# Prompt values of the first two key tiles: three products of rounded numbers and remainders in place of one native float32 product

## The chip, the cores and the metric

The kernel runs on one core of one Trainium2 chip. The metric is the device time of one launch in microseconds (us). TensorE (PE) multiplies into PSUM, VectorE (DVE) and ScalarE (ACT) work on PSUM and SBUF, GpSimd (POOL) on SBUF, and SyncE (SP) issues most transfers.

## The reference

One inference step of a decoder with a gated short-convolution layer and a latent-attention layer, for a prompt of 512 tokens and 8 sample sequences of 8 new tokens each (against 1024 cached ones), model width 2048, 16 heads. The part that the change touches is the prompt's causal attention and its values:

```python
def prompt_latent_attention(q_lat, q_pe, ckv, kpe):
    ...
        p = jax.nn.softmax(sc, axis=-1).astype(ckv.dtype)
        return jnp.einsum('bhqk,bkc->bqhc', p, ckv)
...
def mla_output(o_lat, z, w_kv_up, w_out):
    b, t = o_lat.shape[:2]
    o = jnp.einsum('bthc,chv->bthv', o_lat, w_kv_up[..., QK_NOPE_DIM:]).reshape(b, t, D_ATTN)
    return (o * jax.nn.silu(z)) @ w_out
```

The kernel computes the same thing for the prompt in another order: it first expands the latent into keys and values per head (V = ckv times the value half of w_kv_up), then multiplies the 512 values of a head by its probabilities.

## The kernel before

A float32 number can be fed to PE in two ways. As `F32` it is multiplied natively. As `F32R` PE takes a rounded number; for full precision the kernel then stores a rounded part (hi) and a remainder (lo) and adds three products, hi x hi, hi x lo and lo x hi. Nearly all of the kernel is done in the second way. The prompt's values, the transposes and the sample queries are native.

The prompt's attention runs over `Fori(0, H // G)`: four groups of G = 4 heads. A group makes queries (query_tiles, L1307), keys (key_tiles, L1277) and values (value_tiles, L1291) of its heads, and then goes through the heads. PE's order is written out by hand:

```python
                value_tiles(n + 5, 1)
                scores(1)
                turn_probs(0)
                scores(2)
                values(0)
                turn_probs(1)
                scores(3)
                values(1)
                turn_probs(2)
                sample_queries(0)
                sample_queries(1)
                values(2)
                turn_probs(3)
                sample_queries(2)
                sample_queries(3)
                values(3)
```

For a head j:
- scores(j) (L1336): for each of QT = 4 query tiles i, five rounded products into PSUM bank i, over (i + 1) x 128 keys. Bank i must have been read by the exponentials of head j - 1 (`exp_done`).
- maxima(j) on DVE (L2737): mask of the diagonal block, then the row maximum, for each i; it raises `bias_ready`.
- exps(j) on ACT (L1956): the exponential of each i into `PROBS[j % 2]` with the row sum; it raises `exp_done`. For j >= 2 the buffer must be free, which before the change means that the transposes of head j - 2 are done (`tr_done`).
- normalise(j) on DVE (L2747): reciprocal and four scalings of the probabilities, then `p_ready`.
- turn_probs(j) on PE (L1353): the ten 128 x 128 blocks of the causal triangle are transposed into PSUM banks 4 to 6.
- evac(j) on ACT (L1965): three copies of those banks into `PT` (`pt_evac`).
- values(j) on PE (L1369): for each key tile k = 0 to 3 one native product of 128 values by the probabilities of the query tiles k to 3, that is 512, 384, 256 and 128 columns, accumulated in PSUM bank 7; then `pv_done`. Bank 7 must have been read by out(j - 1) (`o_done`).
- out(j) on DVE (L2756): bank 7 times the gate.
- sample_queries(j) on PE (L1326) takes `WK[j]`, which SP loads (load_wk, L684), one semaphore for each of four buffers.

DVE's order in a group is: remainders of queries and keys, then for j = 0 to 3 maxima(j), normalise(j) and for j >= 2 out(j - 2); then sample_query(0), sample_query(1), out(2), sample_query(2), sample_query(3), out(3). ACT's is: exps(0), two roundings of weights, four copies of PSUM banks 4 to 7 into `V` (L1977, `v_evac`), then exps(1), evac(0), exps(2), evac(1), exps(3), evac(2), evac(3). Engines work through their lists strictly in order, so an instruction that waits holds all behind it.

Of the kernel before, what the change touches and what calls it, by code (L numbers as in the profile page):

```python
# [45 lines left out]
G = 4  # L46
# [105 lines left out]
def build(nc, wstream, adastream, x_in, small_in, cos_in, sin_in, pages, ptab, wk_in, wv_in,  # L152
          y_out, cst_out, ckv_out, kpe_out, rope_park, y_park):
    with ExitStack() as ctx:
# [106 lines left out]
        PROBS = [at(f"probs{i}", ro + 10 * P * i, [P, 10 * P]) for i in range(2)]  # L261
        PRS = at("probs_sample", to, [P, PAST])
# [154 lines left out]
        wk_landed = [sem(f"wk_landed{i}") for i in range(G)]  # L417
# [32 lines left out]
        def _(sp):  # L450
# [233 lines left out]
            def load_wk(h, s):  # L684
                sp.dma_start(WK[s][:, :], wk_in[bass.ds(h, 1), :, :].rearrange("a p n -> p (a n)")).then_inc(wk_landed[s], 16)
# [23 lines left out]
            def group_loads(g, n, last):  # L709
# [11 lines left out]
                for j in range(0 if last else G):  # L721
                    sp.wait_ge(qlat_done, g * G + (j + 1))
                    load_wk(g * G + (j + G), j)
# [99 lines left out]
        def _(pe):  # L823
# [451 lines left out]
            with pe.Fori(0, H // G) as g:  # L1275
# [50 lines left out]
                def sample_queries(j):  # L1326
# [3 lines left out]
                    pe.wait_ge(wk_landed[j], g * 16 + 16)  # L1330
# [22 lines left out]
                def turn_probs(j):  # L1353

                    pe.wait_ge(p_ready, g * G + (j + 1))
                    if j == 0:
                        pe.wait_ge(v_evac, g * G + G)
                    else:
                        pe.wait_ge(pt_evac, g * 12 + 3 * j)
                    s = 0  # L1360
# [8 lines left out]
                def values(j):  # L1369
                    pe.wait_ge(o_done, g * G + (j + BEGUN))  # L1370
                    s = 0
                    for k in range(QT):
                        if k < 3:
                            pe.wait_ge(pt_evac, g * 12 + (3 * j + k + 1))
                        w = QT - k
                        last = pe.matmul(PS[:, 7, k * P:TP], V[:, k, j * VD:(j + 1) * VD], PT[:, s * P:(s + w) * P],  # L1376
                                         start=(k == 0), stop=(k == QT - 1))
                        s += w
                    last.then_inc(pv_done, 1)
# [169 lines left out]
        def _(act):  # L1549
# [389 lines left out]
            with act.Fori(0, H // G) as g:  # L1939
# [16 lines left out]
                def exps(j):  # L1956
                    if j >= 2:
                        act.wait_ge(tr_done, g * 12 + 3 * (j - 1))
# [6 lines left out]
                def evac(j):  # L1965
                    for c in range(3):
                        w = 4 * P if c < 2 else 2 * P
                        act.wait_ge(tr_done, g * 12 + (3 * j + c + 1))
                        act.activation(PT[:, 4 * c * P:4 * c * P + w], PS[:, 4 + c, 0:w], ACT.Copy).then_inc(pt_evac, 1)
# [6 lines left out]
                for t in range(QT):  # L1976
                    act.activation(V[:, t, :], PS[:, 4 + t, :], ACT.Copy).then_inc(v_evac, 1)  # L1977
# [81 lines left out]
        def _(dve):  # L2059
# [676 lines left out]
            def group(g, last=False):  # L2736
# [18 lines left out]

                def out(j):  # L2756
# [18 lines left out]
                for j in range(G):  # L2775
                    maxima(j)
                    normalise(j)
                    if j >= 2:
# [3 lines left out]
                out(2)  # L2782
                sample_query(2)
# [281 lines left out]
```

## Time and profile before

| | |
|---|---|
| median of 3 runs | 2016.57 us (2015.34 to 2018.63) |
| profiled execution | 2017.29 us |
| its span, first to last instruction | 2015.6 us |
| mean granted TensorE clock | 0.992 |
| PE busy | 1951.2 us (97%) |
| DVE busy | 1421.8 us (71%) |
| ACT busy | 848.1 us (42%) |
| POOL busy | 172.3 us (9%) |

The span is what the profile sees; the execution's own time is 1.7 us longer. Times in the rows count from the first instruction. An engine is busy while one of its instructions runs; ends of pipelined matmuls are modelled, so the step from one start to the next is the better measure of what a matmul costs. The granted clock of TensorE has two levels here, 1.00 (2.4 GHz) and 0.50 (1.2 GHz).

### The profile page before, as it was taken

To read this page: it belongs to the slowest core of one execution; us is meant where nothing else is said; L and a number is where in the kernel's file an instruction comes from. 1 tells how busy PE (TensorE), PEld (TensorE's weight loads), DVE (VectorE), ACT (ScalarE), POOL (GpSimd) and SP (SyncE) were. 2 spreads that over 40 slices of the span, in tenths; PEclk is the share of its full clock that TensorE was granted. 3 is DMA by queue.
4 is the path that set the end of the run, shared out by engine and by line. 5 is a ranking of instruction groups with operands and counts; after the bars stand their busy time and mean duration, and the time that the engine had idled before them with its cause. 6 is when DMAs were issued, how large, how long until landed. Compare 5 with 4: busy or idle time off the path is not lost.

```text
span 2015.6 us, 42249 instructions
## 1 busy us (share of the span) xinstructions
PE 1951.2 (97%) x16142; PEld 1836.6 (91%) x16142; DVE 1421.8 (71%) x2077; ACT 848.1 (42%) x1318; POOL 172.3 (9%) x124
## 2 busy tenths in 40 slices
PE   4999999999999999999999999998999999999997
PEld 3899999999999999999999999998888887779996
DVE  5597777777777777797778986676434456669776
ACT  3243333333333333354455634445443444456443
POOL 1200000000000000000000240003221122200002
PEclk8999999999999999999999999999999999999998
DMA  9976555555555565645453434448323239852447
GB/s 392 404 267 210 201 193 193 193 195 204 202 205 198 205 202 197 235 165 159 142 210 138 165 130 139 140 136 299 117 73 94 76 107 347 289 186 96 137 149 282
DMA packets 134902, 386.69 MB, mean 192 GB/s; under 512 B 13906, under 2 KB 44498, under 8 KB 131858
## 3 DMA queue, kind: packets, MB, share of 16 engines
q1 hardware_dynamic: 129682, 368.52, 53.1%
q0 software_dynamic: 5120, 16.78, 2.7%
q8 instruction: 69, 1.13, 0.2%
q14 instruction: 31, 0.25, 0.0%
HBM read 353.92 MB, written 31.33 MB: 191 GB/s over the span
## 4 chain that ended last, share of the span: by engine, by line
PE 82%; DVE 8%; DMA 6%; issue 2%; ACT 1%; SPq 1%; DVEq 0%; ACTq 0%
PE ps L954 36%; PE ps L958 18%; DMA s<-adastream 4%; PE ps L906 3%; PE ps L1435 3%; PE ps L840 3%; PE ps L1286 2%; PE ps L1301 2%; PE ps L1461 2%; PE ps L1319 2%; PE ps L1376 2%; PE ps L892 1%; PE ps L847 1%; DMA w_raw<-wstream 1%; DVE w_split L2177 1%
## 5 line engine op out<-in xcount | busy, mean ns | idle before, releaser
L1617 ACT ACTIVATE w_split<-w_raw 128x1024 fp32r<-128x1024 f32 x204 | 216.0, 1059 | 381.3 <-PE ps L958 207.6
L2177 DVE TENSOR_TENSOR w_split<-w_raw,w_split 128x1024 fp32r<-128x1024 f32 x212 | 259.6, 1224 | 139.2 <-ACT w_split L1617 134.5
L954 PE MATMUL ps<-operand_hi,w_split 128*128 128x288 f32 x1224 | 328.5, 295 | 0.0
L954 PE MATMUL ps<-operand_lo,w_split 128*128 128x288 f32 x1224 | 328.3, 294 | 0.0
L954 PE MATMUL ps<-t_hi,w_split 128*128 128x288 f32 x960 | 262.9, 300 | 1.2 <-ACT w_split L1617 0.7
L954 PE MATMUL ps<-t_lo,w_split 128*128 128x288 f32 x960 | 258.0, 295 | 0.0
L784 POOL TENSOR_TENSOR w_split<-w_raw,w_split 128x1024 fp32r<-128x1024 f32 x47 | 126.3, 2687 | 1509.4 <-ACT w_split L1555 1509.4
L954 PEld LDWEIGHTS ps<-operand_hi,w_split 128*128 128x128 f32 x1224 | 229.7, 188 | 0.1
L954 PEld LDWEIGHTS ps<-operand_lo,w_split 128*128 128x128 f32 x1224 | 229.7, 188 | 0.0
L954 PEld LDWEIGHTS ps<-t_hi,w_split 128*128 128x128 f32 x960 | 180.3, 188 | 10.7 <-issue 8.9
L958 PE MATMUL ps<-operand_hi,w_split 128*128 128x288 f32 x1224 | 186.9, 295 | 0.9 <-DVE w_split L2177 0.9
L954 PE MATMUL ps<-t_hi_out,w_split 128*128 128x288 f32 x672 | 182.2, 297 | 4.8 <-DVE t_lo_out L2430 1.9
L954 PE MATMUL ps<-t_lo_out,w_split 128*128 128x288 f32 x672 | 180.5, 295 | 0.0
L954 PEld LDWEIGHTS ps<-t_lo,w_split 128*128 128x128 f32 x960 | 180.3, 188 | 0.0
L958 PEld LDWEIGHTS ps<-operand_hi,w_split 128*128 128x128 f32 x1224 | 170.2, 188 | 1.5 <-DVE w_split L2177 1.5
L1617 ACT ACTIVATE w_split<-a 128x1024 fp32r<-128x1024 f32 x88 | 93.4, 1061 | 185.1 <-PE ps L958 185.1
L958 PE MATMUL ps<-t_hi,w_split 128*128 128x288 f32 x960 | 146.2, 294 | 0.0
L954 PEld LDWEIGHTS ps<-t_hi_out,w_split 128*128 128x128 f32 x672 | 126.2, 188 | 9.3 <-issue 8.6
L958 PEld LDWEIGHTS ps<-t_hi,w_split 128*128 128x128 f32 x960 | 133.1, 188 | 0.0
L954 PEld LDWEIGHTS ps<-t_lo_out,w_split 128*128 128x128 f32 x672 | 126.2, 188 | 0.0
L2177 DVE TENSOR_TENSOR w_split<-a,w_split 128x1024 fp32r<-128x1024 f32 x88 | 107.4, 1220 | 25.3 <-ACT w_split L1617 25.2
L1555 ACT ACTIVATE w_split<-w_raw 128x1024 fp32r<-128x1024 f32 (+1 forms) x62 | 64.0, 1033 | 130.8 <-PE ps L1319 40.9
(412 smaller groups left out, 3896.6 us busy)
## 6 DMA issues: line engine op xcount, KB each, us to landing
w_raw<-wstream SPq DMA_DIRECT2D x169, 512.0 KB, 3.7
ada_ring<-adastream SPq DMA_DIRECT2D x112, 512.0 KB, 4.6
a<-wstream SPq DMA_DIRECT2D x88, 512.0 KB, 4.7
s<-wstream SPq DMA_DIRECT2D x44, 512.0 KB, 3.4
ada_first_ring<-adastream SPq DMA_DIRECT2D x32, 512.0 KB, 9.2
ada_third<-adastream SPq DMA_DIRECT2D x32, 512.0 KB, 6.4
tiles<-y_park SPq DMA_DIRECT2D x12, 1152.0 KB, 7.3
x_residual<-x_in SPq DMA_DIRECT2D x8, 1152.0 KB, 8.7
```

The source lines that it names most:

```text
L784: pool.tensor_tensor(WL[:, n.slot, 0:width], WR[:, n.slot, 0:width], WH[:, n.slot, 0:width].bitcast(F32), ALU.subtract).then_inc(w_lo_read ...
L840: pe.matmul(PS[0:cols, banks[a], 0:HALF], WH[:, c.slot, kk * cols:(kk + 1) * cols], x[:, k * T + a * HALF:k * T + (a + 1) * HALF], start=( ...
L906: last = pe.matmul(PS[32 * g:32 * g + 32, bank, col:col + P], small("c", 32 * k, 32), w, start=(clears and k == 0), stop=(k == KT - 1), sk ...
L954: pe.matmul(PS[:, bank, 0:HALF], WH[:, c.slot, k * P:(k + 1) * P], x(k), start=(first and k == 0 and x is hi), stop=False, skip_group_chec ...
L958: done = pe.matmul(PS[:, bank, 0:HALF], WL[:, c.slot, k * P:(k + 1) * P], hi(k), start=False, stop=(last and k == HK - 1), skip_group_chec ...
L1286: last = pe.matmul(PS[:, 2 * c + jj, :], w[:, nn.slot, k * 256 + jj * P:k * 256 + (jj + 1) * P], x[:, k * TP:(k + 1) * TP], start=(w is WH ...
L1301: last = pe.matmul(PS[:, 4 + t, :], x[:, k * TP + t * P:k * TP + (t + 1) * P], w[:, nn.slot, kk * 512:(kk + 1) * 512], start=(w is WH and ...
L1319: last = pe.matmul(PS[:, 4 * c + 2 * jj + a, 0:HALF], w[:, nn.slot, k * 256 + jj * P:k * 256 + (jj + 1) * P], x[:, k * T + a * HALF:k * T ...
L1435: pe.matmul(*form(c, k, slice(0, P)), start=(k == 0), stop=False)
L1555: act.activation(WH[:, n.slot, 0:width], WR[:, n.slot, 0:width], ACT.Copy).then_inc(w_hi_ready, 1)
L1617: act.activation(WH[:, c.slot, :], raw, ACT.Copy).then_inc(w_hi_ready, 1)
L2177: dve.tensor_tensor(WL[:, c.slot, :], raw, WH[:, c.slot, :].bitcast(F32), ALU.subtract).then_inc(w_lo_ready, 1)
```

## The change

In values(j), the products of key tiles 0 and 1 are now made of rounded parts: `VH` (values, rounded by ACT when it copies them from PSUM) and `VL` (their remainder), `PTH` (transposed probabilities, rounded by ACT) and `PTL` (their remainder). Key tiles 2 and 3 stay native. With it:
- DVE gets values_low(), four subtractions of 256 columns in each group, between normalise(0) and maxima(1), and probs_low(j), two subtractions of 512 and 384 columns for each head, between normalise(j + 1) and the next out, and for the last head behind out(2).
- ACT's evac(j) copies four pieces, since bank 5 holds columns of both kinds.
- PE waits for `v_lo` before turn_probs(0), since that overwrites the banks from which values_low() reads, and for `p_lo` at the head of values(j).
- `PTL[0]` and `PTL[1]` lie in the memory of `PROBS[0]` and `PROBS[1]`. So exps(j) now waits for values(j - 2) to be done, where it waited for the transposes of head j - 2.
- The four semaphores `wk_landed` become two, each for a pair of `WK` buffers. SP loads the buffers in pairs.

```diff
--- before.py
+++ after.py
@@ -259,6 +259,11 @@
         T2 = at("tmp2", to + T, [P, T])
         ACC = at("acc", to + 2 * T, [P, T])
         PROBS = [at(f"probs{i}", ro + 10 * P * i, [P, 10 * P]) for i in range(2)]
+        PTH = at("probs_t_hi", xo, [P, 7 * P], F32R)
+        PTL = [at(f"probs_t_lo{i}", ro + 10 * P * i, [P, 7 * P], F32R) for i in range(2)]
+        VH = at("values_hi", po + 10496, [P, 2, G * VD], F32R)
+        VL = [[at(f"values_lo{k}{i}", o, [P, 2 * VD], F32R) for i, o in enumerate(places)]
+              for k, places in enumerate(((xo + 4352, po + 14080), (ro + 20 * P, mo + CT * P)))]
         PRS = at("probs_sample", to, [P, PAST])
         PRN = at("probs_new", to + PAST, [P, TS])
         RA21 = at("a21", to, [P, CH])
@@ -414,7 +419,7 @@
         qpe_landed = sem("qpe_landed")
         ckv_stored, ckv_back = sem("ckv_stored"), sem("ckv_back")
         q_hi, q_lo, k_hi, k_lo = sem("q_hi"), sem("q_lo"), sem("k_hi"), sem("k_lo")
-        wk_landed = [sem(f"wk_landed{i}") for i in range(G)]
+        wk_landed, v_lo, p_lo = [sem(f"wk_landed{i}") for i in range(2)], sem("v_lo"), sem("p_lo")
         v_evac = sem("v_evac")
         qlat_done, qlat_evac = sem("qlat_done"), sem("qlat_evac")
         score_done, bias_ready, exp_done, p_ready = sem("score_done"), sem("bias_ready"), sem("exp_done"), sem("p_ready")
@@ -682,7 +687,7 @@
                     b1_back(8 + 4 * g, 12 + 4 * g)
 
             def load_wk(h, s):
-                sp.dma_start(WK[s][:, :], wk_in[bass.ds(h, 1), :, :].rearrange("a p n -> p (a n)")).then_inc(wk_landed[s], 16)
+                sp.dma_start(WK[s][:, :], wk_in[bass.ds(h, 1), :, :].rearrange("a p n -> p (a n)")).then_inc(wk_landed[s // 2], 16)
 
             def load_rope(g, turns, s):
 
@@ -719,7 +724,7 @@
                     sp.wait_ge(rope_parked[1], 128)
                     load_rope(g + 1, 2, 0)
                 for j in range(0 if last else G):
-                    sp.wait_ge(qlat_done, g * G + (j + 1))
+                    sp.wait_ge(qlat_done, g * G + (j // 2 * 2 + 2))
                     load_wk(g * G + (j + G), j)
 
             with sp.Fori(0, H // G - 1) as g:
@@ -1327,7 +1332,7 @@
 
 
                     pe.wait_ge(exp_done, g * 16 + (4 * (G - 1) + j + 1))
-                    pe.wait_ge(wk_landed[j], g * 16 + 16)
+                    pe.wait_ge(wk_landed[j // 2], g * 32 + 32)
                     for k in range(CT):
                         last = pe.matmul(PS[:, j, k * P:(k + 1) * P], WK[j][:, k * P:(k + 1) * P],
                                          QNS[:, j, :], start=True, stop=True)
@@ -1355,8 +1360,10 @@
                     pe.wait_ge(p_ready, g * G + (j + 1))
                     if j == 0:
                         pe.wait_ge(v_evac, g * G + G)
+                        pe.wait_ge(v_lo, g * 2 + 2)
                     else:
                         pe.wait_ge(pt_evac, g * 12 + 3 * j)
+                        pe.wait_ge(p_lo, g * G + j)
                     s = 0
                     for k in range(QT):
                         for i in range(k, QT):
@@ -1368,14 +1375,21 @@
 
                 def values(j):
                     pe.wait_ge(o_done, g * G + (j + BEGUN))
+                    pe.wait_ge(p_lo, g * G + (j + 1))
                     s = 0
                     for k in range(QT):
                         if k < 3:
                             pe.wait_ge(pt_evac, g * 12 + (3 * j + k + 1))
-                        w = QT - k
-                        last = pe.matmul(PS[:, 7, k * P:TP], V[:, k, j * VD:(j + 1) * VD], PT[:, s * P:(s + w) * P],
-                                         start=(k == 0), stop=(k == QT - 1))
-                        s += w
+                        c = slice(s * P, (s + QT - k) * P)
+                        v = slice(j * VD, (j + 1) * VD)
+                        if k < 2:
+                            low = VL[k][j // 2][:, j % 2 * VD:(j % 2 + 1) * VD]
+                            terms = ((VH[:, k, v], PTH[:, c]), (VH[:, k, v], PTL[j % 2][:, c]), (low, PTH[:, c]))
+                        else:
+                            terms = ((V[:, k, v], PT[:, c]),)
+                        for i, (value, prob) in enumerate(terms):
+                            last = pe.matmul(PS[:, 7, k * P:TP], value, prob, start=(k == 0 and i == 0), stop=(k == QT - 1))
+                        s += QT - k
                     last.then_inc(pv_done, 1)
 
                 pe.wait_ge(qlat_evac, g * G + BEGUN)
@@ -1955,7 +1969,7 @@
 
                 def exps(j):
                     if j >= 2:
-                        act.wait_ge(tr_done, g * 12 + 3 * (j - 1))
+                        act.wait_ge(pv_done, g * G + (j - 1 + BEGUN))
                     for i in range(QT):
                         o, w = P * (i * (i + 1) // 2), (i + 1) * P
                         act.wait_ge(bias_ready, g * 16 + (4 * j + i + 1))
@@ -1966,7 +1980,12 @@
                     for c in range(3):
                         w = 4 * P if c < 2 else 2 * P
                         act.wait_ge(tr_done, g * 12 + (3 * j + c + 1))
-                        act.activation(PT[:, 4 * c * P:4 * c * P + w], PS[:, 4 + c, 0:w], ACT.Copy).then_inc(pt_evac, 1)
+                        high = (w, 3 * P, 0)[c]
+                        if high:
+                            last = act.activation(PTH[:, 4 * c * P:4 * c * P + high], PS[:, 4 + c, 0:high], ACT.Copy)
+                        if high < w:
+                            last = act.activation(PT[:, 4 * c * P + high:4 * c * P + w], PS[:, 4 + c, high:w], ACT.Copy)
+                        last.then_inc(pt_evac, 1)
 
                 for s in range(2):
                     act.wait_ge(rope_parked[s], 128)
@@ -1974,7 +1993,7 @@
                 for c in range(2):
                     round_w(n + (4 + c))
                 for t in range(QT):
-                    act.activation(V[:, t, :], PS[:, 4 + t, :], ACT.Copy).then_inc(v_evac, 1)
+                    act.activation((VH if t < 2 else V)[:, t, :], PS[:, 4 + t, :], ACT.Copy).then_inc(v_evac, 1)
                 for j in range(1, G):
                     exps(j)
                     evac(j - 1)
@@ -2753,6 +2772,22 @@
                         last = dve.tensor_scalar(pr, pr, MX[:, 12 + i:13 + i], None, ALU.mult)
                     last.then_inc(p_ready, 1)
 
+                def values_low():
+                    for k in range(2):
+                        dve.wait_ge(v_evac, g * G + (k + 1))
+                        for i in range(2):
+                            c = slice(2 * i * VD, 2 * (i + 1) * VD)
+                            last = dve.tensor_tensor(VL[k][i][:, :], PS[:, 4 + k, c], VH[:, k, c].bitcast(F32), ALU.subtract)
+                        last.then_inc(v_lo, 1)
+
+                def probs_low(j):
+                    dve.wait_ge(tr_done, g * 12 + (3 * j + 3))
+                    for c, w in enumerate((4 * P, 3 * P)):
+                        dve.wait_ge(pt_evac, g * 12 + (3 * j + c + 1))
+                        o = slice(4 * c * P, 4 * c * P + w)
+                        last = dve.tensor_tensor(PTL[j % 2][:, o], PS[:, 4 + c, 0:w], PTH[:, o].bitcast(F32), ALU.subtract)
+                    last.then_inc(p_lo, 1)
+
                 def out(j):
                     dve.wait_ge(pv_done, g * G + (j + 1 + BEGUN))
                     o = B1[:, bass.ds(g * (G * T) + j * T, TP)]
@@ -2775,11 +2810,16 @@
                 for j in range(G):
                     maxima(j)
                     normalise(j)
+                    if j == 0:
+                        values_low()
+                    else:
+                        probs_low(j - 1)
                     if j >= 2:
                         out(j - 2)
                 sample_query(0)
                 sample_query(1)
                 out(2)
+                probs_low(3)
                 sample_query(2)
                 sample_query(3)
                 if last:
```

## Rows read from the trace of the kernel before

**Rows 1.** The page: busy time of PE, and shares of the chain that ended last, by engine.

```profile
PE 1951.2 (97%) x16142; PEld 1836.6 (91%) x16142; DVE 1421.8 (71%) x2077; ACT 848.1 (42%) x1318; POOL 172.3 (9%) x124
...
PE 82%; DVE 8%; DMA 6%; issue 2%; ACT 1%; SPq 1%; DVEq 0%; ACTq 0%
```

**Rows 2.** Windows, one group's tail: length, busy us of PE, PEld, DVE, ACT, POOL, clock, DMA.

```profile
1438.64:1464.89 26.25, 26.24 (x166) 22.07 (x164) 16.70 (x46) 15.22 (x41) 2.40 (x1) 1.00 0.36 93
```

**Rows 3.** Timeline of PE there: start us, us, engine, line, operation, tiles, count.

```profile
1444.44 0.34 PE L1347 MATMUL ps<-k_nope_hi,q_nope_lo 128*128 128x384 f32 x1
1444.61 0.34 PE L1348 MATMUL ps<-k_nope_lo,q_nope_hi 128*128 128x384 f32 x1
...
1445.15 0.40 PE L1346 MATMUL ps<-k_nope_hi,q_nope_hi 128*128 128x512 f32 x1
1445.38 0.40 PE L1347 MATMUL ps<-k_nope_hi,q_nope_lo 128*128 128x512 f32 x1
...
1446.31 2.32 PE L1376 MATMUL ps<-probs_t,values 128*128 128x512 f32 x8
1448.47 1.26 PE L1364 MATMUL ps<-small,probs 128*128 128x128 f32 x10
...
1452.74 2.32 PE L1376 MATMUL ps<-probs_t,values 128*128 128x512 f32 x8
1454.90 1.25 PE L1364 MATMUL ps<-small,probs 128*128 128x128 f32 x10
...
1457.78 2.32 PE L1376 MATMUL ps<-probs_t,values 128*128 128x512 f32 x8
1459.93 1.25 PE L1364 MATMUL ps<-small,probs 128*128 128x128 f32 x10
...
1464.89 0.38 PE L1319 MATMUL ps<-q_latent_hi,w_split 128*128 128x288 f32 x1
```

**Rows 4.** Timeline of ACT there; in brackets the idle time before and its releaser.

```profile
1439.81 2.04 ACT L1977 ACTIVATE values<-ps 128x512 f32<-128x512 f32 x4
1441.72 0.39 ACT L1962 ACTIVATE probs<-ps,row_stats 128x128 f32<-128x128 f32 x1
...
1443.66 0.22 ACT L1962 ACTIVATION_READ_ACCUMULATOR probs<-ps,row_stats 128x1 f32 x1
1443.76 1.38 ACT L1969 ACTIVATE probs_t<-ps 128x512 f32<-128x512 f32 x3
...
1454.55 0.69 ACT L1962 ACTIVATE probs<-ps,row_stats 128x512 f32<-128x512 f32 x1 [0.26 <-DVE row_stats L2745]
```

**Rows 5.** Timeline of DVE there.

```profile
1424.86 1.29 DVE L2773 TENSOR_TENSOR k_nope_lo<-ps,k_nope_hi 128x512 fp32r<-128x512 f32 x2 [3.48 <-ACT k_nope_hi L1953]
...
1439.35 0.30 DVE L2744 TENSOR_TENSOR ps<-ps,small 128x128 f32<-128x128 f32 x1 [7.93 <-PE ps L1351]
...
1451.50 0.29 DVE L2744 TENSOR_TENSOR ps<-ps,small 128x128 f32<-128x128 f32 x1
...
1453.82 0.69 DVE L2745 TENSOR_REDUCE row_stats<-ps 128x1 f32<-128x512 f32 x1
1455.36 0.18 DVE L2749 RECIPROCAL row_stats<-row_stats 128x4 f32<-128x4 f32 x1 [0.85 <-ACT probs L1962]
...
1456.76 0.69 DVE L2759 TENSOR_TENSOR tiles<-ps,tiles 128x512 f32 x1
...
1460.24 0.69 DVE L2759 TENSOR_TENSOR tiles<-ps,tiles 128x512 f32 x1 [1.73 <-PE ps L1376]
```

**Rows 6.** Timeline of PE at two long idle times, and the clock behind one.

```profile
896.76 0.37 PE L954 MATMUL ps<-t_hi_out,w_split 128*128 128x288 f32 x1 [1.89 <-DVE t_lo_out L2430]
...
1366.53 0.37 PE L1263 MATMUL ps<-q_latent_hi,w_split 128*128 128x288 f32 x1 [2.17 <-ACT w_split L1555]
...
896.70:900.20 3.50, 3.44 (x26) 3.47 (x27) 3.36 (x5) 2.73 (x7) 0.00 (x0) 1.00 0.09 32
...
1367.50:1370.90 3.40, 3.40 (x16) 3.40 (x15) 1.17 (x2) 3.14 (x5) 1.48 (x2) 0.50 0.56 169
```

## Prediction

> **What bounds the kernel now.** I read the page first. TensorE (PE) is busy 97% of the span, and the chain of work that ended last runs over PE for 82% of it [rows 1]. That is an average; what this edit is worth is decided in the stretch that it touches. The windows view of the tail of one group (from the second head's scores to the next group's first query product) shows PE busy 26.24 of 26.25 us at full clock, VectorE (DVE) only 16.70 and ScalarE (ACT) 15.22 [rows 2]. There are four such tails, alike to 0.1 us, and the list of waits names no wait of PE in any of them. So PE sets the time there, and any new wait of PE is paid in full unless PE time comes off in the same place. I then read the timelines of PE, ACT and DVE through one tail, because DVE and ACT work in a chain with PE (scores, maxima, exponentials, normalisation, transposes, values) and their slack against PE decides, not their busy share.
>
> **What the three products save.** values(j) takes 2.16 us in the trace: 1446.31 to the next PE group at 1448.47, for 512+384+256+128 = 1280 columns, so 1.69 ns a column [rows 3]. The first two key tiles are 896 columns: 1.51 us. A rounded product starts 0.23 us after the one before it at 512 columns and 0.17 at 384 [rows 3]; I take 0.175, as further such pairs have up to 0.18. Three of each are 3 x (0.23 + 0.175) = 1.21 us. Saving: 0.30 us a head, 1.2 us a group, 4.8 us in all. Weight loads lie beside the products for both forms. As bounds I take 0.25 and 0.37 us a head, the steps read 0.01 us too short or too long by the rounding of the rows and a little for the change of form.
>
> A page speaks for a larger saving. The Trainium skill, "TensorE: Matmul & The Clock Gate", section "Back-to-back issue gap", gives about 131 ns for a stream of 512-column products; the rows have 0.23 us. By the page the three 512-column products alone would save a further 0.3 us a head, an estimate of 4.7 us over sixteen heads. The trace has this very form of product, so the row stands.
>
> **What is added, and where it lies.** Take 0.04 us for a handover between engines: the last maximum of head 3 ends 1453.82 + 0.69 = 1454.51, its exponential starts 1454.55 [rows 4, 5]. The steps are worked in the first group's clock.
>
> The pieces, each from a row. Maxima of a head on DVE, unhindered: 1451.50 to 1454.51 = 3.01 us. Exponentials of a head on ACT back to back: 1441.72 to 1443.66 + 0.22 = 2.16 us [rows 4, 5]. Normalisation to the next DVE instruction: 1455.36 to 1456.76 = 1.40 us. out(j): 0.69 us. After values(j), its result is taken 1460.24 - 1459.93 = 0.31 us behind the start of PE's next group [rows 3, 5]. The new DVE subtraction isn't in the trace for this tile, but k_nope_lo is the same form (PSUM minus rounded copy, 512 columns, fp32r out): two take 1.29 us, so 0.60 to 0.65 each [rows 5]. A step of DVE in PSUM takes 0.30 us at 128 columns and 0.69 at 512 [rows 5], which makes 0.43 at 256, and the next starts some 0.1 before it ends. I take 0.60 and 0.47 us (start to start) for 512 and 384 columns, the last ending 0.56 after its start: 1.16 us until p_lo, 1.07 until DVE's next. Bounds for the pair: below, the normalisation, whose five instructions run over 1280 columns in 1.40 us, pro rata and less its reciprocal about 0.8; above, two of out(j) end to end, 1.38. ACT's evacuation of three pieces (1.38 us [rows 4]) becomes four; some 0.1 us more, behind the exponentials and, as computed, always before DVE is ready for it. That is nil on the path.
>
> Step 1, values_low before maxima(1). DVE waits for ACT's first values copy (four in 2.04 us from 1439.81, so the first by 1440.40 [rows 4]), then has four 256-column subtractions at 0.33: DVE is free at 1441.76. It used to begin maxima(1) at 1439.35. Maxima end 1444.77, the last exponential starts 1444.81 and ends 0.80 later at 1445.61. PE wants it for the last query tile of scores(2) at 1445.15 [rows 3], which takes 1.16 us to 1446.31, and gets it at 1445.65: **wait 0.50 us**; scores(2) ends at 1446.81.
>
> Step 2, p_lo before values(0). normalise(1) starts 1445.65, DVE is free 1447.05, probs_low(0) is done 1448.21. values(0) starts 1448.25: **wait 1.44 us**. Queued behind it on PE are the transposes of head 1 and scores(3).
>
> Step 3, the round trip. Because the remainders share memory with the probabilities, exps(2) may start only after values(0), where it used to need the transposes alone. values(0) ends 1448.25 + 1.86 = 1450.11; ACT starts 1450.42 and ends 1452.58; normalise(2) starts 1452.62, DVE free 1454.02; probs_low(1) to 1455.09; out(0), which values(1) needs for its PSUM bank, to 1455.78. values(1) starts 1455.82. PE itself arrives 1450.11 + (1452.74 - 1448.47) = 1454.38: **wait 1.44 us**.
>
> Step 4, the same again with head 3. values(1) ends 1457.68; ACT 1457.99 to 1460.15; normalise(3) from 1460.19, free 1461.59; probs_low(2) 1462.66; out(1) 1463.35; values(2) starts 1463.39. PE arrives 1457.68 + 2.88 (ten transposes, two sample queries: 1457.78 - 1454.90) = 1460.56: **wait 2.83 us**.
>
> Step 5, none. probs_low(3) ends about 1467.7, PE arrives at values(3) at 1465.25 + 2.88 = 1468.1.
>
> Sum of a group: 0.50 + 1.44 + 1.44 + 2.83 - 1.20 = +5.0 us. Four groups: **+20.0 us**. The same bookkeeping with the old order and waits gives no wait of PE and the end within 0.1 us of 1464.89 [rows 3]. With the bounds of the subtraction and the saving it is +3.9 to +5.7 a group.
>
> The weight loads of SP for the sample queries now come in pairs. They are taken in the next group, some 50 us later; the last pair still leaves at the same qlat_done, and the raw chunk queued behind it had over 5 us before ACT could take it. Nothing. After the last group the sample stage simply starts later: PE goes straight into its scores there, so nothing is given back.
>
> **The clock.** A wait of this size may cost more than itself. Before 1366.53 PE sat idle 2.17 us, and from 1367.5 to 1370.9 the granted clock was 0.50, the 1.2 GHz level; 1.89 us of idle at 896.76 left it at 1.00 [rows 6]. A stretch of 3.4 us at half clock costs up to 1.7 us. The 2.83 us of step 4 is above the idle that lowered it once, but here it stands between busy stretches, and the rows don't show such a case: I take two of the four groups, +3.4 us. Bounds 0 and 4 x 1.7 = 6.8.
>
> **Total.** +23.4 us. On the profiled execution (2017.29 us, span 2015.6 and 1.7 around it) that is 2040.7; on the median of the runs, 0.7 lower, 2016.57 + 23.4 = **2040.0 us**.
>
> **Rivals.** (A) Faster: the saving alone. If DVE's subtractions and the later exponentials stay behind PE's own scores and transposes, 2016.6 - 4.8 = 2011.8 us. For it: DVE is idle 9.5 of 26 us in the tail. Against: that idle lies elsewhere; out(1) ended 1456.76 + 0.69 = 1457.45 and values(2) started 1457.78, so 0.33 us of slack against some 6 us of added chain. It decides only if the chain per head pair is under 0.3 us. (B) The round trip doesn't bind (exps not held by values), only DVE's added work does: the same bookkeeping gives 3.75 a group, +15, 2031.6. (C) The clock never falls: +20.0, 2036.6. (D) It falls in every group: +26.8, 2043.4. (E) The edit doesn't do what it says: three rounded products run no faster than the native one, so no saving: 6.2 a group, +24.8; with the clock as forecast 2044.8. Against: scores use just such operands at 0.17 and 0.23. (F) The waits shrink to the saving and cancel: about 2016.6; nothing in the rows speaks for that.
>
> **Chances.** Forecast (waits as worked, clock down in one to three groups) 0.56; C 0.18; D 0.12; B 0.06; E 0.03; A 0.03; F 0.02. A change under 0.2% (4 us) can't be told from none here. Faster 0.03, same 0.02, slower 0.95. The range takes B's 2031.6 less a little for the lower bound of the subtraction (+3.9 x 4 = 15.6, 2032.2) and on the other side 5.7 x 4 = 22.8 with the clock down in all four, +29.6, 2046.2: **2031 to 2046**, which leaves out A, F and a rest.
>
> **What would show it.** In the profile after, PE's list of waits should have, four times each: about 0.5 us in scores (behind exponentials), 1.4 us before values(0) behind probs_low, 1.4 and 2.8 us before values(1) and values(2) behind out(0) and out(1), none before values(3). ACT's exponentials of heads 2 and 3 should wait 3.6 to 4.2 us for values. The tail should last 31.2 us or more, and values(j) 1.86. If values(j) isn't shorter, E holds; if exps(2) starts before values(0) ends, step 3 is wrong. The forecast fails if DVE reaches out(0) and out(1) much sooner than worked, or if the clock answers to the waits in another way.

## The result, and the profile after

The changed kernel takes 2043.72 us (median of 4 runs, 2043.03 to 2045.14) against 2017.11 before (4 runs): a ratio of 1.0133, 95% interval 1.0121 to 1.0146. That is 26.6 us slower, where 23.4 was forecast, and inside the forecast range of 2031 to 2046. The profiled execution took 2045.14 us with a span of 2043.4.

The page after, the lines that answer to [rows 1]: busy time, and shares of the chain that ended last.

```profile
PE 1957.8 (96%) x16174; PEld 1848.3 (90%) x16174; DVE 1442.4 (71%) x2125; ACT 848.0 (42%) x1334; POOL 172.1 (8%) x124
...
PE 80%; DVE 9%; DMA 5%; issue 3%; ACT 2%; SPq 1%; DVEq 0%; ACTq 0%
```

PE is still busy 96% of the span, and has lost only two points of the chain; DVE, ACT and issue have gained one each. Nothing on this page looks wrong; the loss is seen only in the stretch itself. The windows view after shows three stretches: the tail of group 0, the tail of group 1, and a piece of group 1's (length, then busy us of PE, PEld, DVE, ACT, POOL, granted clock, DMA share, GB/s):

```profile
1439.82:1471.63 31.81, 26.31 (x174) 23.31 (x172) 21.79 (x58) 15.14 (x45) 2.40 (x1) 1.00 0.24 66
1510.01:1543.42 33.41, 27.89 (x174) 24.68 (x172) 21.79 (x58) 15.13 (x45) 2.39 (x1) 0.95 0.24 62
1535.57:1538.98 3.41, 3.41 (x13) 3.02 (x12) 0.26 (x2) 0.00 (x0) 0.00 (x0) 0.50 0.00 1
```

Against the 26.25 us of [rows 2], group 0's tail lasts 31.81 us: +5.56. PE's busy time is 26.31 where it was 26.24, so what is added is idle time of PE. DVE has 5.1 us more work. The tails of groups 1 to 3 last 33.41, 33.43 and 33.49 us, 1.6 more, and in each the granted clock fell to 0.50 (1.2 GHz) for 3.4 us. The stretches between the tails are as before (38.38 us). PE's list of waits over the whole span, behind those of the start:

```profile
PE ps L1391 <- DVE tiles L2794: 16.0, 8, 2.7
PE ps L1391 <- DVE probs_t_lo L2788: 5.5, 4, 1.4
```

Neither existed before. L1391 is values(j), L2794 out(j) and L2788 the subtraction of probs_low(j). The numbers are the total in us, the count and the longest: eight waits for out and four for the remainder, in total 21.5 us. PE's timeline in group 0, the answer to [rows 3]:

```profile
1446.80 0.50 PE L1351 MATMUL ps<-k_nope_hi,q_nope_hi 128*128 128x512 f32 x1
...
1449.57 0.49 PE L1391 MATMUL ps<-probs_t_hi,values_hi 128*128 128x512 f32 x1 [1.35 <-DVE probs_t_lo L2788]
1449.90 0.39 PE L1391 MATMUL ps<-probs_t_lo,values_hi 128*128 128x512 f32 x1
1450.13 0.39 PE L1391 MATMUL ps<-probs_t_hi,values_lo 128*128 128x512 f32 x1
1450.36 0.34 PE L1391 MATMUL ps<-probs_t_hi,values_hi 128*128 128x384 f32 x1
...
1450.89 0.81 PE L1391 MATMUL ps<-probs_t,values 128*128 128x256 f32 x4
1451.54 1.26 PE L1371 MATMUL ps<-small,probs 128*128 128x128 f32 x10
...
1457.27 0.50 PE L1391 MATMUL ps<-probs_t_hi,values_hi 128*128 128x512 f32 x1 [1.30 <-DVE tiles L2794]
...
1464.98 0.49 PE L1391 MATMUL ps<-probs_t_hi,values_hi 128*128 128x512 f32 x1 [2.69 <-DVE tiles L2794]
...
1469.75 0.47 PE L1391 MATMUL ps<-probs_t_hi,values_hi 128*128 128x512 f32 x1
```

The waits stand before values(0), (1) and (2), and values(3) has none. values(0) lasts 1449.57 to 1451.54 = 1.97 us, 0.19 less than the 2.16 of [rows 3]: the first product of the six takes 0.33 us, its two followers 0.23 each. That first product stands behind a wait, which matters below. ACT's timeline shows the round trip (the exponentials wait until values has been done), DVE's the two kinds of subtraction:

```profile
1451.82 0.37 ACT L1976 ACTIVATE probs<-ps,row_stats 128x128 f32<-128x128 f32 x1 [3.76 <-PE ps L1391]
...
1459.53 0.37 ACT L1976 ACTIVATE probs<-ps,row_stats 128x128 f32<-128x128 f32 x1 [4.25 <-PE ps L1391]
```

```profile
1441.59 1.42 DVE L2780 TENSOR_TENSOR values_lo<-ps,values_hi 128x256 fp32r<-128x256 f32 x4 [9.01 <-ACT values_hi L1996]
1442.93 0.29 DVE L2763 TENSOR_TENSOR ps<-ps,small 128x128 f32<-128x128 f32 x1
...
1448.18 1.15 DVE L2788 TENSOR_TENSOR probs_t_lo<-ps,probs_t_hi 128x512 fp32r<-128x512 f32 x2
...
1456.46 0.68 DVE L2794 TENSOR_TENSOR tiles<-ps,tiles 128x512 f32 x1
```

The exponentials of heads 2 and 3 start 0.28 us behind the start of PE's next group after values(0) and values(1) (1451.82 after 1451.54), and had waited some 4 us for it. maxima(1) starts at 1442.93, 3.1 us into the tail, where it started 0.7 into it before [rows 5]: 1.34 of these 2.4 us are the four subtractions, the rest is DVE's wait for ACT's first copy of the values.

Where the 27.8 us between the two spans went: 4 x 5.56 = 22.2 in the tails at full clock (the fourth is 0.08 longer in both kernels), 3 x 1.6 = 4.8 in the clock, and a remainder of under 1 us from two differences outside, of opposite sign (+1.2 ahead of the first tail, -0.5 behind the last). The +1.2 is an execution's chance: a wait near 897 us was 2.45 us long there instead of 1.89 and was followed by half clock. In the traces of the experiments, with that part unchanged, the first tail starts anywhere from 1436.8 to 1440.4 us (1438.6 before, 1439.8 after).

### The profile page after: what moved, and what is told of

Read it like the earlier page. It is cut to its first block, busy times and chain, and to the rows that moved or that the text cites. A ratio compares the mean times of both kernels' runs of the same rounds, so it can differ in the third digit from the quotient of the medians.

```text
span 2043.4 us, 42443 instructions
## 1 busy us (share of the span) xinstructions
PE 1957.8 (96%) x16174; PEld 1848.3 (90%) x16174; DVE 1442.4 (71%) x2125; ACT 848.0 (42%) x1334; POOL 172.1 (8%) x124
## 4 chain that ended last, share of the span: by engine, by line
PE 80%; DVE 9%; DMA 5%; issue 3%; ACT 2%; SPq 1%; DVEq 0%; ACTq 0%
PE ps L959 36%; PE ps L963 18%; DMA s<-adastream 3%; PE ps L911 3%; PE ps L1449 3%; PE ps L845 3%; PE ps L1475 2%; PE ps L1291 2%; PE ps L1306 2%; PE ps L1324 2%; PE ps L1391 2%; PE ps L897 1%; PE ps L852 1%; DMA w_raw<-wstream 1%; DVE w_split L2196 1%
```

## The experiments

Tail means the stretch of [rows 2] in group 0 unless another is named. Medians stand beside those of the kernel before on the same chip.

**1. The products alone.** Edit of the changed kernel:

```diff
-                        pe.wait_ge(v_lo, g * 2 + 2)
...
-                        pe.wait_ge(p_lo, g * G + j)
...
-                    pe.wait_ge(p_lo, g * G + (j + 1))
...
-                            terms = ((VH[:, k, v], PTH[:, c]), (VH[:, k, v], PTL[j % 2][:, c]), (low, PTH[:, c]))
+                            terms = ((VH[:, k, v], PTH[:, c]), (VH[:, k, v], PTH[:, c]), (VH[:, k, v], PTH[:, c]))
...
-                        act.wait_ge(pv_done, g * G + (j - 1 + BEGUN))
+                        act.wait_ge(tr_done, g * 12 + 3 * (j - 1))
...
-                    if j == 0:
-                        values_low()
-                    else:
-                        probs_low(j - 1)
...
-                probs_low(3)
```

> The three rounded products alone: each is VH x PTH (leaves out both remainders, counts the rounded product three times), no subtraction on DVE, no p_lo or v_lo wait, and the exponentials wait for the transposes as before the change. Theory (the loss is PE waiting for DVE and for the round trip, the products themselves gain): values(j) takes 1.97 us in place of 2.16, so 16 x 0.19 = 3.0 us faster than before, about 2014, ratio 0.9985, no new wait of PE and a tail of 25.5 us. Rival (the twelve instruction records in place of eight, or the mixed forms, cost PE time): slower than before, a tail over 26.25 us.

Measured: 2012.48 us (10 runs) against 2016.93, ratio 0.9980 (0.9970 to 0.9989). The windows view of group 1's tail:

```profile
1504.36:1529.73 25.37, 25.35 (x174) 23.47 (x172) 16.64 (x46) 15.35 (x45) 2.39 (x1) 1.00 0.32 82
```

PE is full again, in 25.37 us for 26.25. Over the four tails (25.59, 25.37, 25.36, 25.47) it gains 3.3 us. The products gain, as the theory has it, and the rival is out. PE's timeline of values(0) in group 0 shows more:

```profile
1448.04 1.38 PE L1387 MATMUL ps<-probs_t_hi,values_hi 128*128 128x512 f32 x6
1449.26 0.82 PE L1387 MATMUL ps<-probs_t,values 128*128 128x256 f32 x4
```

The six products take 1.22 us, and values(0) lasts 1.87 in all, to the transposes at 1449.91; values(1) also lasts 1.87. With no wait ahead of it a head thus saves 0.29 us, not the 0.19 on which the expectation rested. The tail gains less than four times that, because the saving of the first two heads is more than the 0.33 us of slack before values(2): PE now waits there for out(1), by its timeline 0.22 us in group 0.

**2. The waits and subtractions alone.** Edit of the changed kernel:

```diff
-                        if k < 2:
+                        if k < 0:
...
-                            last = act.activation(PTH[:, 4 * c * P:4 * c * P + high], PS[:, 4 + c, 0:high], ACT.Copy)
+                            last = act.activation(PT[:, 4 * c * P:4 * c * P + high], PS[:, 4 + c, 0:high], ACT.Copy)
...
-                    act.activation((VH if t < 2 else V)[:, t, :], PS[:, 4 + t, :], ACT.Copy).then_inc(v_evac, 1)
+                    act.activation(V[:, t, :], PS[:, 4 + t, :], ACT.Copy).then_inc(v_evac, 1)
...
-                            last = dve.tensor_tensor(VL[k][i][:, :], PS[:, 4 + k, c], VH[:, k, c].bitcast(F32), ALU.subtract)
+                            last = dve.tensor_tensor(VL[k][i][:, :], PS[:, 4 + k, c], V[:, k, c], ALU.subtract)
...
-                        last = dve.tensor_tensor(PTL[j % 2][:, o], PS[:, 4 + c, 0:w], PTH[:, o].bitcast(F32), ALU.subtract)
+                        last = dve.tensor_tensor(PTL[j % 2][:, o], PS[:, 4 + c, 0:w], PT[:, o], ALU.subtract)
```

> The waits and DVE's subtractions alone: values and transposed probabilities are copied unrounded and multiplied natively as before the change, but DVE subtracts and PE and ACT wait as after it (the computation is whole). Theory: a group loses what it loses after the change and the saving of 0.19 x 4 on top, so a tail of 26.25 + 5.56 + 0.76 = 32.6 us and +25.3 us in all, with the clock down in three groups another 4.8: 2042 to 2048, most likely 2047. Rival (the products cost the time): within 1 us of before, 2017.

Measured: 2043.60 us against 2016.93, ratio 1.0139 (1.0124 to 1.0155). Windows of the tail, and PE's timeline of values(0):

```profile
1437.04:1469.99 32.95, 27.47 (x165) 22.01 (x164) 21.80 (x58) 15.11 (x45) 2.40 (x1) 1.00 0.23 66
```

```profile
1446.80 2.42 PE L1391 MATMUL ps<-probs_t,values 128*128 128x512 f32 x8 [1.34 <-DVE probs_t_lo L2788]
```

All four tails last 32.95 to 33.04 us, at full clock in this execution: +6.7 each, 26.8 in all, with the same waits (1.34, 1.30, 2.69 us) as the changed kernel. The whole loss is in the dependencies and DVE's work, none in the products. It is 0.35 us a tail more than expected. The native values(0), (1) and (2) behind their waits last 2.26, 2.25 and 2.25 us (values(0) from 1446.80 to 1449.06), where the kernel before, without waits, has 2.16: a values group of either form costs 0.10 us more behind a wait. The clock part of the expectation missed: waits as long left it at 1.00 in the profiled execution (one of the other three, at 2048.72 us and a mean clock of 0.988, looks like one in which it fell).

**3. No values_low.** Edit of the changed kernel:

```diff
-                        pe.wait_ge(v_lo, g * 2 + 2)
...
-                            terms = ((VH[:, k, v], PTH[:, c]), (VH[:, k, v], PTL[j % 2][:, c]), (low, PTH[:, c]))
+                            terms = ((VH[:, k, v], PTH[:, c]), (VH[:, k, v], PTL[j % 2][:, c]), (VH[:, k, v], PTH[:, c]))
...
-                    if j == 0:
-                        values_low()
-                    else:
+                    if j:
```

> The changed kernel without values_low and its wait; the third product takes the rounded value again (leaves out the values' remainder). Theory (a chain: DVE late for maxima(1) makes exponentials, scores(2) and probs_low(0) late): the wait before values(0) falls from 1.35 to about 0.35 us, the 0.5 us in scores(2) goes, the waits before values(1) and values(2) stay at 1.3 and 2.7. 1.6 us a group less than the changed kernel, +20 of before with the clock falling as there, about 2037. Rival (values_low is covered by DVE's idle time): as the changed kernel, 2044.

Measured: 2035.57 us against 2016.93, ratio 1.0089 (1.0074 to 1.0105). Windows of the tail of group 1, whose clock stayed up, and PE's waits:

```profile
1507.66:1537.81 30.15, 25.90 (x174) 23.34 (x172) 20.76 (x54) 14.70 (x45) 2.39 (x1) 1.00 0.26 67
```

```profile
PE ps L1389 <- DVE tiles L2792: 16.0, 8, 2.7
...
PE ps L1389 <- DVE probs_t_lo L2786: 1.0, 4, 0.3
```

30.15 us is 1.66 less than the changed kernel's 31.81. The four waits for probs_low have shrunk from 5.5 us to 1.0, the eight for out are the same to 0.1 us. So most of the 2.4 us by which maxima(1) is late in the changed kernel reached values(0) through the exponentials, scores(2) and probs_low(0), and was not covered by DVE's idle time. The clock fell in three of the four tails (31.60 to 31.78 us), as expected.

**4. No probs_low.** Edit of the changed kernel (the exponentials still wait for the values):

```diff
-                        pe.wait_ge(p_lo, g * G + j)
...
-                            terms = ((VH[:, k, v], PTH[:, c]), (VH[:, k, v], PTL[j % 2][:, c]), (low, PTH[:, c]))
+                            terms = ((VH[:, k, v], PTH[:, c]), (VH[:, k, v], PTH[:, c]), (low, PTH[:, c]))
...
-                    else:
-                        probs_low(j - 1)
...
-                probs_low(3)
```

> The changed kernel without probs_low and its waits; the second product takes the rounded probabilities again (leaves out the probabilities' remainder). exps(j) still waits for values(j - 2). Theory: the round trip through the shared buffer stays, DVE's 1.07 us before each out goes: +2.1 us a group, waits before values(1) and values(2) of about 0.3 and 1.8 us, none of them long enough for the clock, +8.5 us, 2025.6. Rival (the round trip is nothing, the subtractions are all): +1.3 us a group at most, values_low's part, about 2022; second rival (round trip is all): as the changed kernel, 2044.

Measured: 2023.49 us against 2016.93, ratio 1.0034 (1.0020 to 1.0047); tails of 28.04 to 28.15 us, 1.8 over before (2.1 expected). PE's waits:

```profile
PE ps L1389 <- DVE tiles L2792: 7.5, 8, 1.6
```

The time, 6.6 us over before, lies nearer the first rival's 2022 than the 2025.6 expected; the list of waits tells them apart: a wait of 1.6 us before values(2) remains, which values_low alone doesn't make. The expected 2.1 a group leaves out the 0.50 us of step 1 and the saving; with both the prediction's bookkeeping gives +1.4. probs_low is worth 3.8 us a group.

**5. The round trip undone.** Edit of the changed kernel:

```diff
-        PTL = [at(f"probs_t_lo{i}", ro + 10 * P * i, [P, 7 * P], F32R) for i in range(2)]
+        PTL = [at(f"probs_t_lo{i}", xo + 6912 + 11 * P * i, [P, 7 * P], F32R) for i in range(2)]
...
-                                    for x in (QNH, QNL) if w is WH else (QNH,):
+                                    for i, x in enumerate((QNH, QNH) if w is WH else (QNH,)):
...
-                                                         start=(w is WH and k == 0 and x is QNH),
+                                                         start=(w is WH and k == i == 0),
...
-                        act.wait_ge(pv_done, g * G + (j - 1 + BEGUN))
+                        act.wait_ge(tr_done, g * 12 + 3 * (j - 1))
```

> The changed kernel with the probabilities' remainders in memory of their own (that of q_latent_lo; the query products take the rounded latent in its place, so the queries are not those of the reference, at the same instructions), and exps(j) waiting for the transposes of head j - 2 as before the change. Theory: the round trip ends, DVE's added work stays: waits before values(0), (1), (2) of 1.4, 0.6 and 2.1 us, 4.0 us a group in place of 5.4, so +16 us and up to 1.6 for each group in which a 2.1 us wait lowers the clock: 2033 to 2039. Rival (DVE's work alone binds, the memory shared is nothing): as the changed kernel, 2044. Second rival (the round trip is all): about 2014.

Measured: 2034.08 us against 2016.38, ratio 1.0091 (1.0074 to 1.0108). Windows of the tail, and PE's waits:

```profile
1438.37:1468.51 30.14, 26.33 (x174) 23.32 (x172) 21.81 (x58) 15.77 (x45) 2.40 (x1) 1.00 0.25 71
```

```profile
PE ps L1391 <- DVE tiles L2794: 9.3, 8, 1.9
...
PE ps L1391 <- DVE probs_t_lo L2788: 5.4, 4, 1.4
```

+3.9 us a group in place of 5.56: memory of its own would take back less than a third. In group 1 the clock fell behind the 1.91 us wait before values(2), and that tail lasts 31.83. Both rivals are out.

**6. The round trip alone.** Edit of the kernel before:

```diff
-                        act.wait_ge(tr_done, g * 12 + 3 * (j - 1))
+                        act.wait_ge(pv_done, g * G + (j - 1 + BEGUN))
```

> The kernel before with one edit: exps(j) waits for values(j - 2), not for the transposes (native products, no subtraction, whole computation). Theory (the round trip costs by itself, through normalise and out): waits of PE of 0.3 us before values(1) and 1.8 us before values(2), +2.1 us a group, no fall of the clock, +8.2 us, 2025. Rival (DVE's idle time covers the later exponentials, so only with the subtractions does the trip bind): within 1 us of before, 2017.

Measured: 2026.33 us against 2017.74, ratio 1.0047 (1.0030 to 1.0064). Windows of the tail, and PE's waits:

```profile
1438.69:1467.32 28.63, 26.76 (x166) 22.08 (x164) 16.59 (x46) 14.43 (x41) 2.38 (x1) 1.00 0.31 84
```

```profile
PE ps L1376 <- DVE tiles L2759: 7.4, 8, 1.6
```

One changed wait on ACT, with no work added anywhere, costs +2.4 us a group. The prediction's bookkeeping has +2.1.

**7. out(j - 2) ahead of probs_low(j - 1).** Edit of the changed kernel:

```diff
+                    if j >= 2:
+                        out(j - 2)
                     if j == 0:
                         values_low()
                     else:
                         probs_low(j - 1)
-                    if j >= 2:
-                        out(j - 2)
```

> The changed kernel with out(j - 2) ahead of probs_low(j - 1) on DVE. Both must be done before values(j - 1), so by the theory nothing moves: waits of 1.3 and 2.7 us before values(1) and (2), now behind probs_low, and 2044 us within 1. Rival (PSUM bank 7, released by out, is what PE waits for, and the subtraction could come later): 1.07 us less at two places of a group, 8.6 us in all, 2035.

Measured: 2044.43 us against 2016.38, ratio 1.0142 (1.0125 to 1.0159); tail 32.02 us (+0.2). PE's waits:

```profile
PE ps L1391 <- DVE probs_t_lo L2788: 22.4, 12, 2.8
```

All twelve waits now bear the name of the subtraction, and their sum is 22.4 for 21.5 us. The name in the list is that of whichever of the two comes last on DVE. The order of the two is worth only these 0.2 us a group, and the new one is the worse.

**8. The clock, with idle products.** Edit of the changed kernel, in a first run with 20, in a second with 10:

```diff
                 sample_queries(1)
+                pe.wait_ge(exp_done, g * 16 + 16)
+                keep_warm(2, 20)
                 values(2)
```

> The changed kernel with twenty idle products (about 2.3 us, into a PSUM bank that is free) before values(2), where PE waits 2.7 us. Theory (the idle of that wait lowers the granted clock for 3.4 us in three of four groups, 1.6 us each): the clock stays at 1.00 in all four groups, each tail is 31.8 us and the time 4.8 us under the changed kernel's, about 2039. Rival (the clock falls for another reason, or the loss there is in the waits): as the changed kernel, 2044, with stretches at 0.50 in the groups; second rival (the idle products themselves are late and push the chain): slower than 2044.

Measured with twenty: 2044.31 us against 2016.38, ratio 1.0141 (1.0124 to 1.0158). Windows of the tail, and its timeline (L1032 is the idle product; each is two records):

```profile
1436.76:1470.08 33.32, 30.51 (x213) 27.69 (x212) 21.80 (x58) 15.13 (x45) 2.40 (x1) 1.00 0.23 61
```

```profile
1459.07 4.63 PE L1032 MATMUL ps<-small 128*128 128x128 f32 x40
1463.45 0.47 PE L1391 MATMUL ps<-probs_t_hi,values_hi 128*128 128x512 f32 x1
```

The clock stayed up in all four tails, but I had taken 0.115 us for a product, which is the price of one record. They lasted 4.4 us instead of 2.3, more than the wait of 2.7 holds, values(2) began 1.5 us late, and this cost what the clock gave: the second rival. So it says nothing yet of the gain, and the number was halved.

> The changed kernel with ten idle products before values(2) in place of twenty. The trace of the run with twenty shows them lasting 4.2 us, 0.21 each, so that values(2) began 1.5 us late; the clock stayed at 1.00 in the groups. Theory: ten last 2.1 us, inside the wait of 2.7; the clock stays up, values(2) begins 25.2 us after the tail's start, all four tails are 31.8 us, 4.8 us under the changed kernel, 2039. Rival (2.1 us of small products don't count as work for the clock, or the wait left over lowers it): stretches at 0.50 behind values(2) and 2044.

Measured with ten: 2038.40 us against 2017.74, ratio 1.0109 (1.0092 to 1.0125), 20.7 us over before where the changed kernel is 26.6 over. Windows of the first two tails and timeline:

```profile
1437.03:1468.83 31.80, 28.51 (x194) 25.53 (x192) 21.80 (x58) 15.14 (x45) 2.40 (x1) 1.00 0.25 68
1507.20:1538.99 31.79, 28.50 (x193) 25.52 (x192) 21.80 (x58) 15.14 (x45) 2.40 (x1) 1.00 0.25 66
```

```profile
1459.34 2.40 PE L1032 MATMUL ps<-small 128*128 128x128 f32 x20
1462.20 0.49 PE L1391 MATMUL ps<-probs_t_hi,values_hi 128*128 128x512 f32 x1 [0.46 <-DVE tiles L2796]
```

All four tails last 31.8 to 31.9 us, together 4.8 less than in the changed kernel. One profile would prove little, as experiment 2 also had none with half clock; but the mean granted clock is 0.992 to 0.993 in all four runs with ten idle products, and 0.988 to 0.990 in all four of the changed kernel.

**9. The paired semaphores alone.** Edit of the kernel before:

```diff
-        wk_landed = [sem(f"wk_landed{i}") for i in range(G)]
+        wk_landed = [sem(f"wk_landed{i}") for i in range(2)]
...
-                    sp.wait_ge(qlat_done, g * G + (j + 1))
+                    sp.wait_ge(qlat_done, g * G + (j // 2 * 2 + 2))
...
-                    pe.wait_ge(wk_landed[j], g * 16 + 16)
+                    pe.wait_ge(wk_landed[j // 2], g * 32 + 32)
```

(and the transfers raise `wk_landed[s // 2]`.)

> The kernel before with only the two semaphores and the paired loads of the sample-query weights. Theory: nothing, 2017 within 1 us, no wait of PE in the tails. Rival (a later weight load or the paired wait holds PE): over 1 us slower, with a wait of PE before a sample query or before the next group's first query product.

Measured: 2017.32 us (10 runs) against 2016.38, ratio 1.0003 (0.9994 to 1.0013), and a tail of 26.25 us without a wait of PE. Nothing, as expected.

## Why the prediction was right

The tails of the runs, in us over the 26.25 of before, at full clock. The first column is the bookkeeping of the prediction, with its own prices, redone for each edit. The second adds what the runs showed and the prediction lacks: 0.10 us for each values group that stands behind a wait, wherever its later end delays what follows.

| | as predicted | with the 0.10 | measured |
|---|---|---|---|
| the change | +5.0 | +5.3 | +5.56 |
| waits and subtractions alone | +6.2 | +6.5 | +6.7 |
| no values_low | +3.3 | +3.6 | +3.9 |
| no probs_low | +1.4 | +1.6 | +1.8 |
| round trip undone | +3.8 | +3.9 | +3.9 |
| round trip alone | +2.1 | +2.3 | +2.4 |
| out ahead of probs_low | +5.0 | +5.3 | +5.8 |

The parts don't add up: taking out values_low gives back 1.7 us, the round trip 1.7, probs_low 3.8, which is more than the whole 5.56. They are links of one chain, and PE pays for the chain's length beyond its own work.

- **PE has no slack.** Right. Each of the seven kernels with a longer chain shows its cost as waits of PE.
- **The saving.** Right in itself: 0.30 us a head was forecast and 0.29 is what experiment 1 shows where nothing waits (six products in 1.22 us, forecast 1.21). At values(3) it is 0.28, sample queries and values taken together: 1468.05 to 1471.63 = 3.58 us after, 1461.03 to 1464.89 = 3.86 before.
- **The term that is missing.** The sum puts at nothing what PE loses when it starts again behind a wait. values(0), (1) and (2) last 1.97 us where 1.86 was forecast, and the native form shows the same 0.10 (experiment 2). This is 0.3 of the 0.56 us by which a tail is longer than the forecast 5.0. More than half of the rest is at values(0), see step 2.
- **Step 1.** 0.50 us in scores(2) forecast. The last query tile of scores(2) starts 6.98 us into the tail (1446.80) where it was 6.51 [rows 3]: 0.47. The list of waits does not name it, where the prediction wanted it to. Experiment 3 shows that the delay comes from values_low.
- **Step 2.** values(0) was forecast 1.94 us late against the tail's start and is 2.08. The subtraction ends at 1448.18 + 1.15 = 1449.33 and values(0) starts 0.24 us later, where 0.04 was taken for a handover.
- **Steps 3 and 4.** values(1) 3.1 forecast, 3.35 found; values(2) 5.6 and 6.0. From the end of one values group over the exponentials, normalise, probs_low and out to the start of the next the prediction has 5.71 us, the trace 5.73 both times, so the chain itself was priced right. The subtractions cost DVE 1.15 us to their end and 1.07 to its next instruction, as taken from k_nope_lo [rows 5]. The profile's own idle figures, 1.30 and 2.69, are smaller, since they count from the modelled end of the matmul before. Experiments 4 to 6 show that DVE's work and the round trip both bind.
- **Step 5.** Right, no wait before values(3).
- **The paired loads.** Nothing, shown by experiment 9.
- **The clock.** Two groups of four were taken; it fell in three, at 1.6 us each, in the profiled execution. The count was a guess, and that it came near is luck: with waits as long, experiment 2 has none. Experiment 8 shows that the clock stays up when the wait before values(2) is filled, and that 4.8 us of the tails hang on it.
- **The page of the Trainium skill.** "TensorE: Matmul & The Clock Gate", section "Back-to-back issue gap", has about 131 ns for a stream of 512-column products. That didn't come: the products of this kernel start 0.23 us apart at that size.
- **Rivals.** B's measured counterpart, the round trip undone, lies at 2034 us, where B said 2031.6. The result lies above the forecast's 2040.0, above C's 2036.6 and nearest to D's 2043.4. But D isn't what happened in the profiled execution: there the clock fell in three groups, and the four tails lost 2.2 us more than worked. A's mechanism is out; its 2011.8 is what the products do alone, 2012.5. They gain 4.5 us by the medians, and with the chain the same products come to lose 26.6.

## What to carry to other kernels

Splitting a native product into rounded parts moves work from the engine that is full to engines that look idle, but they are links of the same chain. Add the new work to the chain between two uses of the full engine, and compare it with the slack there (0.33 us before values(2)), not with busy shares. A buffer that is reused is a dependency even when it costs no instruction: here it was worth 2.4 us a group by itself. A version that beats the kernel before would have to keep all of PE's new waits under 0.8 us a group, which is what the products gain in experiment 1; none of these edits comes near it.

## What the runs showed of the hardware that was not expected

- PE starts again slower behind a wait. Native values groups last 2.25 to 2.26 us behind one and 2.16 without (experiments 2 and 6 against before); with the rounded products it is 1.97 and 1.87 (the changed kernel against experiment 1). In the rounded form the first step shows it, 0.33 us instead of 0.23. values(3) also has 0.32 at its first step, with no wait ahead; but there the sample queries ahead of it take 1.70 us where they took 1.78 before native values, so nothing is lost. Waits before the score tiles show it too: the tile at 1446.80 starts 0.33 us before its follower at 1447.13. Why it is so wasn't tried.
- Waits of 2.69 to 2.70 us were followed by 3.4 us at half clock in three of four groups of the changed kernel and in three of four without values_low, waits of 2.80 in three of four with out moved ahead, and waits of 2.69 to 2.70 in none of four with native products. A wait of 1.91 us was followed by it in one group of four (experiment 5). Near 897 us, in code that no edit touches, a wait of 1.89 us was followed by half clock in four of nine traces, and one of 2.42 us (experiment 6) was not. So the 1.89 us that left the clock up in [rows 6] was one execution's, and no length of wait seen here decides it alone. What does stays open; that work of no use in the wait before values(2) keeps the clock up is shown by experiment 8.
- A native 128-column product is two records of the trace, 0.24 us for the pair (ten idle products in 2.40 us).
